# Paired mixer banks for DeltaNet's heads, norms summed by ScalarE, layer norm in parts, and steps placed anew

## The chip, the cores and the metric

One Trainium2 chip, one of its NeuronCores. The time is the device time of one execution of the kernel in microseconds (us); a kernel's time is the median of its runs. Engines are named as in the profile: PE (TensorE's matmuls), PEld (its weight loads), DVE (VectorE), ACT (ScalarE), POOL (GpSimd), SP (SyncE, which starts most DMAs).

## The reference

Two residual layers on x of 256 tokens x 2048, float32, with 256 memory tokens. Each layer is one input projection of the RMS-normed stream, token mixers on slices of it, a gate for each, and one output projection:

```
even:  p = rms_norm(h) @ w_in                      (2048 x 9232)
  A) q,k,v = silu(causal_conv(p[:3072], 4 taps)), 8 heads of 128
     q,k = l2_norm(q)/sqrt(128), l2_norm(k);  gated delta rule in chunks of 64
     o_a = rms_norm(o) * silu(z_a)
  B) glu = a * sigmoid(b) (1024 wide); c = causal_conv(glu, 31 taps) + bias
     o_b = silu(layer_norm(c)) * silu(z_b)
  M) 4 heads of softmax attention over the memory, times silu(z_m)
  h = h + concat(o_a, o_b, o_m) @ w_out            (3072 x 2048)
odd:   stick-breaking attention (16 heads) and the memory attention, gated,
  h = h + concat(o_c, o_m) @ w_out
```

## The kernel before

**The products.** The weights of all projections are cut into 432 chunks of 256 rows by 512 columns. Each is loaded once by SP into one of six `raw` buffers (`load_chunk`, L716). ACT rounds it to `whi` (L912), DVE takes the remainder `wlo` (L1245), both into rings of seven, and PE multiplies it by the two 128-token halves of x, itself kept as a rounded part `xhi` and a remainder `xlo`: three products for each (L1608, L1609, L1610), 12 matmuls of 128x512 for a chunk, into four PSUM banks. This "job" work goes on from the first microsecond to the last, and PE does the mixers' small products and transpositions (`turn`, L1647) between two chunks.

**The order.** `make_plan` (L155) writes one list of steps for all engines. Position p is the place ahead of chunk p; `stream(k, pos, items)` puts steps from a position on, each item with the distance to the next. Each engine walks through the whole list and does its own part of a step (`do_<step>`), in order, so an engine that waits inside a step holds back everything behind it. The split of a chunk (L912 on ACT, L1245 on DVE) stands 4 positions ahead of its products (`AHEAD`). The 124 tap steps of the 31-tap convolution (L1469, on DVE) are put wherever DVE's estimated time leaves room: `VECTOR_SHARE` and `TENSOR_SHARE` hold estimates in chunks, `CONV_SHARE` is that of a tap step, and `CONV_ROOM` what DVE may be behind.

**Mixer banks.** Four more PSUM banks `M[0]` to `M[3]` take the mixers' results. `banks(step)` (L581) says which a step uses; `take` lets PE wait until the last reader of each is through.

**DeltaNet** (`deltanet(g)`, four heads at a time). For a head: `dnT`, PE turns q, k and v (six blocks of 128x128) into banks 0 and 1; `dnC`, ACT writes the first tap of the 4-tap convolution (L1006) and DVE adds nine more (L1319); `dnS`, ACT's tanh back into banks 0 and 1 (L1012, L1013); `dnU`, DVE makes silu of it (L1327, L1329); `dnB`, POOL squares q and k (L825), PE sums the squares by four one-column products with ones (L1711) and turns k and v back by token (three blocks, L1647), all into bank 2, ACT copies the turned blocks out (L1020), DVE the norms (L1335). Then the factors (`dnV`, `dnR`, `dnG`), the inverse of the chunk's triangular matrix (`inF`, `inT`, and `d4x`/`d4y`: POOL masks a product at L851, PE multiplies at L1748, L1760 and L1762, DVE at L1416), the recurrence (`d5a` to `d5e`), the output's norm (`d6`, with ACT's accumulated squares at L1070), `gate`, and `d7`, which turns the output into the layout that the output projection reads.

**Convolution module.** `glu`, `gT` (turned, ACT's copy at L1084), the tap steps, `lnc` (POOL adds the finished channels, L859), then the layer norm: `lnm` (mean by PE, one subtraction of 2048 columns on DVE, L1476), `lnv` (ACT squares, DVE adds), `lns` and `lnr` (variance, root, reciprocal, and one multiplication of 2048 columns, L1494), `lno` (per 256 columns: gain and bias on DVE, ACT's tanh, DVE's gates).

**Others.** `zT` turns and applies gates (L1509), `xt` turns x or memory and splits it (L949 on ACT, L1266 on DVE, two banks), `mf` moves mixed results into the products' layout. SP starts, ahead of the first chunks, 14 loads of small vectors (L728).

The head loop as it was:

```
for h in range(h0, h0 + 4):
    s += [(("dnT", h), .2), (("dnC", h), 1.2), (("dnS", h), .9),
          (("dnU", h), DN_STEP - (2.1 if h > h0 else 1.7))]
    s += [(("dnB", h - 1), .1)] if h > h0 else []
```

## Time and profile before

| | |
|---|---|
| median of 3 runs | 1384.59 us (1384.58 to 1385.32) |
| the profiled execution | 1385.76 us |
| its span in the profile | 1384.0 us |
| PE busy | 1363.7 us, 99% of the span, 6473 instructions |
| DVE busy | 890.0 us, 64% |
| ACT busy | 753.1 us, 54% |
| POOL busy | 113.1 us, 8% |
| mean granted TensorE clock | 0.995 of full speed |
| DMA | 172 GB/s over the span |

The span is the time from the first to the last instruction of the profiled execution; 1.76 us of that execution lie outside it. Busy time of PE holds matmuls at the throttled clock too, so a busy PE is not one at its peak. An idle time of an engine costs the end only where PE, which has work of its own all the way, is the one that waits.

### The profile page before, as it was taken

The numbers are of one execution on the slowest core, as the hardware profiler recorded it, in microseconds if no ns is written. First come the engines' busy times: TensorE is split into PE (matmuls) and PEld (weight loads), VectorE is DVE, ScalarE is ACT, GpSimd is POOL, SyncE is SP. The second block draws the span as 40 slices with busy tenths as digits, with TensorE's granted clock in tenths as the row PEclk, the third lists the DMA queues.
The fourth block names the chain that finished last, engine by engine and source line by source line (L and its number), as shares of the span: only waits on it lengthen the run. The fifth ranks groups of instructions, "written<-read, shape, count | busy, mean of one in ns | idle before, by whom it ended". The sixth has DMA issues, their size and how long they took to land.

```text
span 1384.0 us, 17368 instructions
## 1 busy us (share of the span) xinstructions
PE 1363.7 (99%) x6473; PEld 1131.6 (82%) x6473; DVE 890.0 (64%) x1327; ACT 753.1 (54%) x1163; POOL 113.1 (8%) x112
## 2 busy tenths in 40 slices
PE   8999999999999999899999999999999999999998
PEld 7788888887888878788888888888888888888887
DVE  5457688887787888665566545654645745556563
ACT  5545543556435564665445455856756757665341
POOL 2001201012210100000000120020020100000000
PEclk9999999999999999999999999999999999999999
DMA  9655545554554675365464655464564564653652
GB/s 291 204 170 167 168 145 179 160 160 152 148 192 136 207 244 181 103 219 162 136 199 151 215 167 193 135 206 151 182 198 149 176 189 141 197 168 122 196 184 76
DMA packets 134477, 239.27 MB, mean 173 GB/s; under 512 B 13904, under 2 KB 19961, under 8 KB 134393
## 3 DMA queue, kind: packets, MB, share of 16 engines
...
HBM read 234.32 MB, written 3.80 MB: 172 GB/s over the span
## 4 chain that ended last, share of the span: by engine, by line
PE 89%; DVE 5%; issue 3%; ACT 2%; DMA 1%; POOL 0%; SPq 0%; DVEq 0%; ACTq 0%; POOLq 0%
PE job L1608 26%; PE job L1610 26%; PE job L1609 26%; PE mixer L1647 3%; DVE wlo L1245 2%; PE mixer L1856 1%; PE mixer L1876 1%; PE mixer L1748 1%; DVE reg L1319 1%; DMA raw<-in_ev_w_in_dram 1%; DVE cvr L1469 1%; PE mixer L1894 1%; PE mixer L1762 1%; PE mixer L1907 0%; PE mixer L1729 0%
## 5 line engine op out<-in xcount | busy, mean ns | idle before, releaser
L1608 PE MATMUL job<-whi,xhi 128*128 128x512 f32 x1724 | 693.4, 402 | 0.0
L1245 DVE TENSOR_TENSOR wlo<-raw,whi 128x1024 fp32r<-128x1024 f32 x432 | 528.4, 1241 | 230.5 <-ACT whi L912 228.0
L1610 PE MATMUL job<-whi,xlo 128*128 128x512 f32 x1724 | 675.6, 392 | 0.0
L1609 PE MATMUL job<-wlo,xhi 128*128 128x512 f32 x1724 | 674.0, 391 | 0.0
L912 ACT ACTIVATE whi<-raw 128x1024 fp32r<-128x1024 f32 x432 | 445.9, 1056 | 143.5 <-PE job L1610 134.9
L1610 PEld LDWEIGHTS job<-whi,xlo 128*128 128x128 f32 x1724 | 325.0, 189 | 70.5
L1609 PEld LDWEIGHTS job<-wlo,xhi 128*128 128x128 f32 x1724 | 326.0, 189 | 63.1
L1608 PEld LDWEIGHTS job<-whi,xhi 128*128 128x128 f32 x1724 | 325.4, 189 | 62.0 <-DVE xlo L1272 0.2
L1469 DVE SCALAR_TENSOR_TENSOR cvr<-cvr,vt 128x255 f32<-128x255 f32 (+14 forms) x240 | 106.9, 501 | 0.0
L939 ACT ACTIVATE proj<-job,rstd 128x512 f32<-128x512 f32 x80 | 50.5, 686 | 51.5 <-PE job L1610 44.2
L1261 DVE TENSOR_TENSOR hid<-hid,job 128x512 f32<-128x512 f32 x48 | 30.7, 681 | 50.1 <-PE job L1610 50.1
L1647 PE MATMUL mixer<-ident,proj 128*128 128x128 f32 x256 | 42.3, 273 | 5.3 <-ACT cvr L1084 2.1
L1647 PEld LDWEIGHTS mixer<-ident,proj 128*128 128x128 f32 x256 | 32.0, 140 | 17.1 <-issue 7.7
L1566 DVE SCALAR_TENSOR_TENSOR scr<-mixer,scr 128x384 f32<-128x384 f32 x16 | 8.9, 557 | 56.4 <-ACT scr L1196 56.4
L1194 ACT ACTIVATE scr<-mixer 128x384 f32<-128x384 f32 x16 | 7.9, 492 | 60.0 <-PE mixer L1894 60.0
L814 POOL TENSOR_TENSOR brs<-bss,mhalf 128x16 f32<-128x16 f32 x4 | 15.2, 3808 | 306.9 <-DVE bss L1560 306.9
L949 ACT ACTIVATE xhi<-mixer,vt 128x256 fp32r<-128x256 f32 x48 | 20.1, 470 | 31.3 <-PE mixer L1647 31.3
L1319 DVE SCALAR_TENSOR_TENSOR reg<-mixer,vt,reg 128x255 f32<-128x255 f32 (+2 forms) x72 | 28.7, 472 | 9.7 <-ACT reg L1006 9.7
L1042 ACT ACTIVATE reg<-mixer 128x512 f32<-128x512 f32 x12 | 7.2, 599 | 42.1 <-PE mixer L1748 42.1
L1121 ACT ACTIVATE mix<-mixer 128x256 f32<-128x256 f32 x40 | 15.1, 377 | 21.4 <-PE mixer L1647 21.4
L851 POOL TENSOR_TENSOR reg<-hid,mix 128x512 f32<-128x512 f32 x12 | 17.9, 1493 | 93.3 <-DVE mix L1377 59.8
L1266 DVE SCALAR_TENSOR_TENSOR xlo<-mixer,vt,xhi 128x256 fp32r<-128x256 f32 x48 | 20.8, 477 | 6.9 <-ACT xhi L949 6.9
...
## 6 DMA issues: line engine op xcount, KB each, us to landing
raw<-in_od_w_in_dram SPq DMA_DIRECT2D x160, 512.0 KB, 4.5
...
```

What stands on the lines that cost most here:

```text
L912: act(whi[:, c % RING, :, :], raw[:, c % RAWS, :, :], ACT.Copy).then_inc(s_hi, 1)
L939: ins = act(dst, pj[j % 2][t][:, :], ACT.Copy, scale=rstd[:, src, t:t + 1])
L949: act(xhi[:, SLOT[n], :], M[banks("xt", n)[0]][:, 0:S], ACT.Copy, scale=xt_gain(n)).then_inc(s_xh, 1)
L1245: vec.tensor_tensor(wlo[:, c % RING, :, :], raw[:, c % RAWS, :, :], whi[:, c % RING, :, :].bitcast(F32), ALU.subtract).then_inc(s_lo, 1)
L1261: ins = vec.tensor_tensor(v, v, pj[j % 2][t][:, :], ALU.add)
L1266: vec.scalar_tensor_tensor(out=xlo[:, SLOT[n], :], in0=M[banks("xt", n)[0]][:, 0:S], scalar=xt_gain(n), in1=xhi[:, SLOT[n], :].bitcast(F32 ...
L1319: vec.scalar_tensor_tensor(out=y[:, r:], in0=dn_source(c)[:, 0:S - r], scalar=vt[:, col:col + 1], in1=y[:, r:], op0=ALU.mult, op1=ALU.add) ...
L1469: ins = vec.scalar_tensor_tensor(out=c[:, d:], in0=gsrc[:, 0:S - d], scalar=vt[:, col:col + 1], in1=c[:, d:], op0=ALU.mult, op1=ALU.add)
L1608: mm(out_, xh, hi, start=first, stop=False)
L1609: mm(out_, xh, lo, start=False, stop=False)
L1610: return mm(out_, xl, hi, start=False, stop=last)
L1647: return nc.tensor.transpose(dst, src, ident[:, :])
```

## The change

- **Banks.** `dnT` and `dnB` of even heads use banks 0 and 1, those of odd heads 2 and 3. A head now takes 3 positions: turns and first taps at the first, the step back by token of the head before and the tanh at the second, silu at the third.
- **Norms.** POOL's squares, PE's one-column products and DVE's copy are gone. PE turns all six blocks back (q's and k's too), and ACT, behind its copy of three of them, takes four squares with an accumulated sum, straight into `nrm`.
- **Outputs.** `d7` of the first four heads stands right behind their gates and goes to banks 2 and 3.
- **Order.** `CONV_SHARE` is .33 for .36, and the `xt` and `mf` steps are placed ahead of the tap steps, so that their DVE time counts when these are levelled; sixteen `xt` steps of the memory stand one to a position, not two; `gT` and the first tap steps move by a position or two.
- **Layer norm in parts.** Subtraction, squares and sum by 512 columns; the gain and the reciprocal in one instruction for 256 columns; the bias by ACT.
- **Start.** Ten warming calls of PE for seven, the gain's transposition (`first`) inside the list behind the first split, eleven small vector loads right behind chunk 0's on SP, without the wait for the first piece of x.

The core of the diff (left out: semaphore names, the tables of steps, and where `M[0]`, `M[1]` become `M[2 * (h % 2)]` and the next):

```diff
-WARM = 7
-DN_STEP = 3.5
+WARM = 10
 BASE, LEVELS = 4, 3
 INV_STEP = (3.0, 3.0)
 CONV_ROOM = 0.2
-CONV_SHARE = 0.36
+CONV_SHARE = 0.33
 ...
-            s += [(("dnT", h), .2), (("dnC", h), 1.2), (("dnS", h), .9), (("dnU", h), DN_STEP - (2.1 if h > h0 else 1.7))]
-            s += [(("dnB", h - 1), .1)] if h > h0 else []
-        s += [("wait", 1), (("dnB", h0 + 3), 1), (("dnV", g), 2), (("dnR", g), 2.5)]
+            s += [(("dnT", h), 0), (("dnC", h), 1)] + ([(("dnB", h - 1), 0)] if h > h0 else [])
+            s += [(("dnS", h), 1), (("dnU", h), 1)]
+        s += [(("dnB", h0 + 3), 1), (("dnV", g), 2), (("dnR", g), 2.5)]
 ...
-        return s, last + [("wait", 1)] + [(("d7", h), 2 - 1.2 * g) for h in range(h0, h0 + 4)]
+        return s, last + [("wait", g)] + [(("d7", h), .5 + .3 * g) for h in range(h0, h0 + 4)]
 ...
+    stream(-1, -1, [(("first", 0), 0)])
 ...
-    start = max(int(p) + 1, after(J_V[1]))
+    start = max(int(p) + 3, after(J_V[1]))
 ...
+        stream(5, CH0[J_MEM] - 11 + k, [(("xt", F_MEM + k), 0)])
+        stream(5, CH0[J_MEM] - 2 + k, [(("xt", F_MEM + 8 + k), 0)])
 ...
-        stream(2, after(J_GLU[g] + 1) + 6 * g, [(("glu", g), 1)] + [(("gT", ct), 1) for ct in range(4 * g, 4 * g + 4)])
+        stream(2, after(J_GLU[g] + 1) + 6 * g, [(("glu", g), 2 + g)] + [(("gT", ct), 1) for ct in range(4 * g, 4 * g + 4)])
 ...
-            if p < after(J_GLU[pr // 2] + 1) + 6 * (pr // 2) + 3 + 2 * (pr % 2):
+            if p < after(J_GLU[pr // 2] + 1) + 7 * (pr // 2) + 4 + 2 * (pr % 2):
 ...
     p = stream(2, p, [(("lnm", 0), 2)])
-    p = int(p) + 1
-    stream(2, p, [(("lnv", a), 0) for a in range(4)])
-    p = stream(2, p + 2, [(("lns", 0), 0), (("lnr", 0), 2)])
-    p = stream(2, max(p, q), [(("lno", ct), .8) for ct in range(8)])
+    p = stream(2, int(p), [(("lnx", 0), .5), (("lnx", 1), .5), (("lnv", 1), .5), (("lnx", 2), .5), (("lnv", 2), .5),
+                           (("lnx", 3), .5), (("lnv", 3), 1)])
+    p = stream(2, p, [(("lns", 0), 0), (("lnr", 0), 2)])
+    p = stream(2, max(p, q), [(("lna", 0), .5)])
+    for ct in range(8):
+        p = stream(2, p, ([(("lna", ct + 1), .4)] if ct < 7 else []) + [(("lno", ct), .5)])
 ...
-        stream(5, CH0[J_MEM] + k - 2, [(("xt", F_MEM + 2 * k), 0), (("xt", F_MEM + 2 * k + 1), 0)])
 ...
-                return [1 if i in (5, 7) else 2]
+                return [2 + i % 2 if i < 4 else 1 if i in (5, 7) else 2]
+            if step in ("dnT", "dnB"):
+                return [0, 1, 2, 3][2 * (i % 2):2 * (i % 2) + 2]
 ...
-            sp.wait_ge(s_xin[0], 16)
+            for dst, src in vecs(vrow)[1:12]:
+                sp.dma_start(dst, src).then_inc(s_vrow, 16)
 ...
-            for dst, src in vecs(vrow)[1:]:
+            for dst, src in vecs(vrow)[12:]:
 ...
-            def do_dnB(h):
-                gp.wait_ge(s_silu, 2 * h + 2)
-                if h:
-                    gp.wait_ge(s_np, h)
-                k = ykqv[:, h % 4, 0:2, :]
-                nc.gpsimd.tensor_tensor(scr[:, 0:512].rearrange("p (c s) -> p c s", c=2), k, k, ALU.mult).then_inc(s_sq, 1)
 ...
-                act(tok[:, h % 4, :, :], M[2][:, 0:384].rearrange("p (c n) -> p c n", c=3), ACT.Copy).then_inc(s_tok, 1)
+                m = M[2 * (h % 2):2 * (h % 2) + 2]
+                act(tok[:, h % 4, :, :], m[1][:, 0:384].rearrange("p (c n) -> p c n", c=3), ACT.Copy).then_inc(s_tok, 1)
+                for a in range(4):
+                    v = m[0][:, 128 * a - 128:128 * a] if a else m[1][:, 0:128]
+                    ins = act(scr[:, 128 * a:128 * a + 128], v, ACT.Square, accum_out=nrm[:, h, a:a + 1])
+                ins.then_inc(s_nrm, 1)
 ...
+            def do_lnx(a):
+                sc.wait_ge(s_xc, a + 1)
+                if a >= 2:
+                    sc.wait_ge(s_lss, a - 1)
+                dst = cvr[:, 8:10, :] if a else scr[:, 512:1024].rearrange("p (c s) -> p c s", c=2)
+                act(dst, cvr[:, 2 * a:2 * a + 2, :], ACT.Square).then_inc(s_lsq, 1)
 ...
+            def do_lna(ct):
+                sc.wait_ge(s_xn, ct + 2)
+                act(cvr[:, ct, :], cvr[:, ct, :], ACT.Identity, bias=gain("ev_ln_b", ct)).then_inc(s_ly, 1)
 ...
-            def do_dnB(h):
-                ve.wait_ge(s_np, h + 1)
-                ve.wait_ge(s_tok, h + 1)
-                vec.tensor_copy(nrm[:, h, :], M[2][:, 384:388]).then_inc(s_nrm, 1)
 ...
-                v = cvr[:, 0:8, :]
-                vec.tensor_tensor(v, v, scr[:, 0:S].unsqueeze(1).broadcast_to([128, 8, S]), ALU.subtract).then_inc(s_xc, 1)
+                v = cvr[:, 2 * a:2 * a + 2, :]
+                vec.tensor_tensor(v, v, scr[:, 0:S].unsqueeze(1).broadcast_to([128, 2, S]), ALU.subtract).then_inc(s_xc, 1)
 ...
-                if a == 0:
-                    vec.tensor_copy(acc, sq).then_inc(s_lss, 1)
-                else:
-                    ve.wait_ge(s_lss, a)
-                    vec.tensor_tensor(acc, acc, sq, ALU.add).then_inc(s_lss, 1)
+                if a > 1:
+                    ve.wait_ge(s_lss, a - 1)
+                vec.tensor_tensor(acc, acc, sq, ALU.add).then_inc(s_lss, 1)
 ...
-                link(vec.reciprocal(r, r))
-                v = cvr[:, 0:8, :]
-                vec.tensor_tensor(v, v, r.unsqueeze(1).broadcast_to([128, 8, S]), ALU.mult).then_inc(s_xn, 1)
-
-            def do_lno(ct):
+                vec.reciprocal(lnacc[:, :], r).then_inc(s_xn, 1)
+
+            def do_lna(ct):
                 ve.wait_ge(s_xn, 1)
                 c = cvr[:, ct, :]
-                vec.tensor_scalar(c, c, gain("ev_ln_g", ct), gain("ev_ln_b", ct), ALU.mult, ALU.add).then_inc(s_ly, 1)
+                vec.scalar_tensor_tensor(out=c, in0=c, scalar=gain("ev_ln_g", ct), in1=lnacc[:, :], op0=ALU.mult, op1=ALU.mult
 ...
-                pe.wait_ge(s_sq, h + 1)
-                for a in range(4):
-                    ins = mm(M[2][:, 384 + a:385 + a], scr[:, 128 * a:128 * a + 128], ones[:, 0:1], start=True, stop=True)
-                ins.then_inc(s_np, 1)
+                m = M[2 * (h % 2):2 * (h % 2) + 2]
                 y = ykqv[:, h % 4, :, :]
-                turn(M[2][:, 0:128], y[:, 0, 0:128])
-                turn(M[2][:, 128:256], y[:, 2, 0:128])
-                turn(M[2][:, 256:384], y[:, 2, 128:256]).then_inc(s_back, 1)
+                turn(m[1][:, 0:128], y[:, 0, 0:128])
+                turn(m[1][:, 128:256], y[:, 2, 0:128])
+                turn(m[1][:, 256:384], y[:, 2, 128:256])
+                turn(m[0][:, 0:128], y[:, 0, 128:256])
+                turn(m[0][:, 128:256], y[:, 1, 0:128])
+                turn(m[0][:, 256:384], y[:, 1, 128:256]).then_inc(s_back, 1)
```

ACT in the first group of heads (`dnC` L1006/L1010, split L912/L911, `dnS` L1012 and L1013/L1016 and L1017, `dnB` L1020/L1025 and L1028), before:

```order
L1006 ACTIVATE reg<-mixer,vt 128x256 x3
L912 ACTIVATE whi<-raw 128x1024
L1012 ACTIVATE mixer<-reg 128x512
L1013 ACTIVATE mixer<-reg 128x256
L939 ACTIVATE proj<-job,rstd 128x512 x2
L912 ACTIVATE whi<-raw 128x1024 x2
L1020 ACTIVATE hid<-mixer 128x384
L912 ACTIVATE whi<-raw 128x1024
```

and in the change, the same stretch, one head:

```order
L1010 ACTIVATE reg<-mixer,vt 128x256 x3
L911 ACTIVATE whi<-raw 128x1024
L1025 ACTIVATE hid<-mixer 128x384
L1028 ACTIVATE scr,nrm<-mixer 128x128 x4
L1016 ACTIVATE mixer<-reg 128x512
L1017 ACTIVATE mixer<-reg 128x256
L911 ACTIVATE whi<-raw 128x1024
L943 ACTIVATE proj<-job,rstd 128x512 x2
L911 ACTIVATE whi<-raw 128x1024
```

The copy for the head before now stands ahead of this head's tanh, with four squares behind it.

POOL where the second four heads' blocks are inverted (a memset of `inF`, `lnc` L859/L858, mask products of `d4x` L851/L850, the power of `d6` L814/L820), before:

```order
L831 MEMSET mix 64x16
L859 TENSOR_TENSOR lnacc<-lnacc,cvr 128x256 x2
L851 TENSOR_TENSOR reg<-hid,mix 128x512 x6
L859 TENSOR_TENSOR lnacc<-lnacc,cvr 128x256 x2
L814 TENSOR_TENSOR oms<-oms,mhalf 128x8
```

and in the change:

```order
L830 MEMSET mix 64x16
L850 TENSOR_TENSOR reg<-hid,mix 128x512 x4
L858 TENSOR_TENSOR lnacc<-lnacc,cvr 128x256 x2
L850 TENSOR_TENSOR reg<-hid,mix 128x512 x2
L820 TENSOR_TENSOR oms<-oms,mhalf 128x8
```

Two additions of the sum for the layer norm have moved from ahead of the six mask products to a place ahead of the last two.

DVE at the layer norm (splits L1245, `xlo` of `xt` L1266, sums L1482 and L1485, L1490 to L1494 the variance's part), before:

```order
L1482 COPY scr<-cvr 128x512
L1485 TENSOR_TENSOR scr<-scr,cvr 128x512 x3
L1266 SCALAR_TENSOR_TENSOR xlo<-mixer,vt,xhi 128x256 x2
L1245 TENSOR_TENSOR wlo<-raw,whi 128x1024
L1266 SCALAR_TENSOR_TENSOR xlo<-mixer,vt,xhi 128x256 x2
L1245 TENSOR_TENSOR wlo<-raw,whi 128x1024
L1490 TENSOR_SCALAR scr<-mixer 128x256
L1492 RECIPROCAL scr<-scr 128x256
L1494 TENSOR_TENSOR cvr<-cvr,scr 128x2048
L1266 SCALAR_TENSOR_TENSOR xlo<-mixer,vt,xhi 128x256 x2
```

and in the change (splits L1254, `xlo` L1278, subtraction L1483, sums L1490, the variance's part L1495 and L1497):

```order
L1254 TENSOR_TENSOR wlo<-raw,whi 128x1024
L1490 TENSOR_TENSOR scr<-scr,cvr 128x512
L1483 TENSOR_TENSOR cvr<-cvr,scr 128x512
L1278 SCALAR_TENSOR_TENSOR xlo<-mixer,vt,xhi 128x256
L1254 TENSOR_TENSOR wlo<-raw,whi 128x1024
L1490 TENSOR_TENSOR scr<-scr,cvr 128x512
L1278 SCALAR_TENSOR_TENSOR xlo<-mixer,vt,xhi 128x256
L1254 TENSOR_TENSOR wlo<-raw,whi 128x1024
L1495 TENSOR_SCALAR scr<-mixer 128x256
L1497 RECIPROCAL lnacc<-scr 128x256
```

The long instructions and the four sums in a row have been cut and stand with a split or two between them.

## Rows read from the trace of the kernel before

**Rows 1.** The page, part 4: the chain that ended last, by engine.

```profile
PE 89%; DVE 5%; issue 3%; ACT 2%; DMA 1%; POOL 0%; SPq 0%; DVEq 0%; ACTq 0%; POOLq 0%
```

**Rows 2.** Waits of PE, 96 to 570 us: us in total, times, longest us.

```profile
PE mixer L1647 <- DVE xlo L1266: 4.0, 2, 2.1
PE mixer L1647 <- ACT cvr L1084: 2.1, 2, 1.9
PE mixer L1647 <- DVE mix L1509: 1.9, 2, 1.4
PE mixer L1647 <- DVE reg L1329: 1.2, 2, 0.9
PE mixer L1748 <- issue: 1.0, 1, 1.0
```

**Rows 3.** Timeline of PE: start us, us, instructions, [idle before <-releaser].

```profile
340.92 0.41 PE L1647 MATMUL mixer<-ident,proj 128*128 128x128 f32 x2 [1.88 <-ACT cvr L1084]
...
492.94 0.39 PE L1610 MATMUL job<-whi,xlo 128*128 128x512 f32 x1
493.79 0.41 PE L1647 MATMUL mixer<-ident,proj 128*128 128x128 f32 x2 [0.46 <-DVE mix L1509]
...
567.54 0.66 PE L1647 MATMUL mixer<-ident,reg 128*128 128x128 f32 x2 [2.14 <-DVE xlo L1266]
```

**Rows 4.** Windows: us, busy us of each engine, PEclk, DMA share, GB/s.

```profile
97.30:144.30 47.00, 46.08 (x227) 38.70 (x226) 36.69 (x61) 27.38 (x42) 4.95 (x3) 1.00 0.54 160
557.00:561.00 4.00, 4.00 (x12) 3.10 (x12) 2.93 (x4) 2.72 (x4) 0.00 (x0) 0.57 0.42 129
700.00:720.00 20.00, 20.00 (x90) 16.57 (x89) 13.16 (x20) 9.31 (x14) 0.00 (x0) 1.00 0.62 199
```

**Rows 5.** Timeline of PE: a head's turns, and a step back by token.

```profile
97.34 0.82 PE L1647 MATMUL mixer<-ident,proj 128*128 128x128 f32 x6
97.92 0.48 PE L1608 MATMUL job<-whi,xhi 128*128 128x512 f32 x1
...
144.34 0.95 PE L1711 MATMUL mixer<-ones,scr 128*128 128x1 f32 x8
145.43 0.47 PE L1608 MATMUL job<-whi,xhi 128*128 128x512 f32 x1
```

**Rows 6.** Timeline of DVE in the layer norm.

```profile
541.81 2.29 DVE L1476 TENSOR_TENSOR cvr<-cvr,scr 128x2048 f32<-128x2048 f32 x1 [0.77 <-ACT scr L1089]
...
564.71 2.29 DVE L1494 TENSOR_TENSOR cvr<-cvr,scr 128x2048 f32<-128x2048 f32 x1
```

**Rows 7.** Timelines of DVE and POOL: splits beside POOL's squares, and without them.

```profile
120.98 1.99 DVE L1245 TENSOR_TENSOR wlo<-raw,whi 128x1024 fp32r<-128x1024 f32 x1
...
126.40 1.21 DVE L1245 TENSOR_TENSOR wlo<-raw,whi 128x1024 fp32r<-128x1024 f32 x1
...
119.94 1.95 POOL L825 TENSOR_TENSOR scr<-reg 128x512 f32<-128x512 f32 x1 [10.76 <-DVE reg L1329]
```

**Rows 8.** Groups of ACT, L1070 of d6: count, busy us, mean ns.

```profile
L1070 ACT ACTIVATE hid<-hid 128x128 f32<-128x128 f32 x8 | 2.4, 302 | 7.2 <-DVE hid L1427 7.2
L1070 ACT ACTIVATION_READ_ACCUMULATOR hid<-hid 128x1 f32 x8 | 1.5, 187 | 0.0
```

**Rows 9.** Timelines of POOL, DVE and PE in the inversion of the second heads.

```profile
373.60 2.54 POOL L859 TENSOR_TENSOR lnacc<-lnacc,cvr 128x256 f32<-128x256 f32 x2 [25.89 <-DVE cvr L1469]
...
412.39 1.46 POOL L851 TENSOR_TENSOR reg<-hid,mix 128x512 f32<-128x512 f32 x1 [3.30 <-DVE mix L1416]
...
412.23 2.68 DVE L1469 SCALAR_TENSOR_TENSOR cvr<-cvr,vt 128x248 f32<-128x248 f32 x4
...
416.77 1.11 PE L1748 MATMUL mixer<-mix,reg 128*128 128x128 f32 x8
```

**Rows 10.** Timelines of ACT and PE at the start.

```profile
18.03 1.06 ACT L912 ACTIVATE whi<-raw 128x1024 fp32r<-128x1024 f32 x1 [1.65 <-DMA raw<-in_ev_w_in_dram]
...
20.89 0.65 PE L1647 MATMUL mixer<-ident,hid 128*128 128x128 f32 x4 [2.00 <-DVE xlo L1266]
```

85 lines of the change are left out of this document (42 added, 43 removed).

## The prediction

> **What bounds the kernel now.** I read first the chain that ended last, then PE's waits, then the timeline around each wait, and windows for the clock. The chain is PE for 89% of the span [rows 1], and PE has its own products from end to end, so the time changes only by what leaves or enters PE's own queue, by idle time of PE, and by its clock. Between 96 and 570 us five groups of waits add up to 4.0 + 2.1 + 1.9 + 1.2 + 1.0 = 10.2 us, in nine waits [rows 2]: the reader is to see that all end with work of the mixers, on DVE or ACT, and none with a weight's split or a load. After 600 us PE is busy throughout (20.00 of 20.00 us in a sample [rows 4]), and from there on the order of both kernels is the same, so the odd layer is worth nothing here.
>
> A wait costs a little more than its idle time. Products start .23 us apart; where 492.94 is followed by a turn at 493.79, .85 - .23 = .62 us are lost, and the row says .46 [rows 3]: .16 for the restart. And three of the waits have a second price. From 557.0 to 561.0 PE does 12 instructions in 4 us, and the granted clock is 0.57 of full speed, that is mostly the lower level (1.2 GHz) [rows 4]; it follows the wait of 1.9 us that ended at 556. Such stretches of about 3.4 us, half of it lost, 1.7 us, stand behind the waits of 1.88 us at 340.92 and of 2.14 us at 567.54 too [rows 3], and one behind the wait of 2.00 us at 20.89 [rows 10]; the waits of up to 1.4 us have none behind them. So a wait of 2 us costs 3.9 us, and one of 1.4 us costs 1.6.
>
> **The change part by part.**
>
> *Norms.* Before, a step back by token takes from 144.34 to 145.43, 1.09 us: four one-column products and three turns [rows 5]. Six turns take from 97.34 to 97.92, .58 us [rows 5]; the step now has six turns. 8 heads x (1.09 - .58) = 4.1 us leave PE's own queue. I take 4.0. This is the surest term, since nothing hides PE's work. POOL's squares go as well: beside one of 1.95 us a split of DVE took 1.99 us in place of 1.21 [rows 7], up to 8 x .78 us that DVE gets back; DVE's copy of .15 us goes too. DVE's time counts only through PE's waits, below.
>
> ACT pays: four squares with their sums, 4 x (302 + 187) ns = 1.96 us a head [rows 8]. In the four heads from 97.3 to 144.3 us ACT was busy 27.4 us beside PE's 47 [rows 4], with 15 splits in it. The change takes 12 positions for them, so about 12 splits: 27.4 - 3 x 1.06 + 4 x 1.96 = 32.1 us, against 12 x 2.73 + 8 x .58 = 37.4 us of PE. It fits. What stands behind the squares in ACT's queue is the tanh, which DVE's nine taps hold back anyway (the taps are at work for 3.5 us behind ACT's first tap, and the squares fill 2.45 us of that with the copy), then splits that are 4 chunks, 11 us, ahead of PE. Cost: nothing; without that cover it is a rival.
>
> *Paired banks.* The turns of a head waited until DVE's silu of the head before had left banks 0 and 1 (reg L1329, 1.2 us in two waits [rows 2]). Now they need the banks of the head before that one, whose last reader is an ACT square a whole head, 3 positions, earlier. Both waits go: 1.2 + 2 x .16 = 1.5 us. The group gets shorter in positions, but every chunk has to be done anyway, so this in itself is worth nothing.
>
> *Order.* The waits for ACT's copy of `gT` (2.1), for DVE's gates of `zT` (1.9) and for the mask product of `d4x` (1.0) are places where DVE or ACT had fallen behind its list; the levelling with .33 for .36 and with the `xt` and `mf` steps counted spreads the taps more evenly, `gT` moves by two positions, `zT` by eight. Adding up durations by position from the groups, I find DVE up to 4.8 us behind at the layer norm before, and under 2 us in the change, everywhere. 5.0 + 5 x .16 = 5.8 us.
>
> *Layer norm in parts.* DVE's two long instructions take 2.29 us each [rows 6], and between them stood four sums that each waited for ACT's squares. `xlo` of the paired `xt` steps, and so PE's next turn, stood behind: the waits of 1.9 and 2.1 us. Cut in four, a subtraction is some .6 us with a split between, the `xt` steps come one to a position, and the bias is ACT's. Both waits should go: 4.0 + 2 x .16 = 4.3 us.
>
> *Clock.* With the waits of 1.88, 1.9 and 2.14 us go three stretches: 3 x 1.7 = 5.1 us.
>
> *What is new.* Two additions on POOL now stand ahead of the last two mask products of the second group. They took 2.54 us [rows 9], and can start only when the last tap of their channels is done; taps start at 412.23 just as POOL starts its product of 1.46 us at 412.39, and PE takes that product at 416.77 [rows 9]. With one tap (.7) and the additions ahead, the product would end at 413.0 + 2.5 + 1.5 = 417.0: .3 late. Bounds: 0 (the taps done one position earlier) and 1.5 (the additions again slowed by DVE, as splits were [rows 7]). I take .4. The mean of the layer norm and the gates of `zT` at new places: .4, between 0 and 1. Together .8.
>
> *Start.* Three more warming calls (some .5 us each at the lower clock, estimated from 128-column turns) and `first` behind the split delay the gain by about 1 us; eleven small loads on SP ahead of the second chunk's cost its issue up to 4.6 us, less the wait removed. Against it, they no longer stand behind the loads. But what PE waits for here is chunk 4, whose split starts at 18.03 when its load has landed [rows 10], with the DMA queues full from 7 to 24 us whatever the order. Net 0, between -2.4 and +.7; the half-speed stretch behind it stays.
>
> The Trainium skill bears on one place. The DVE row beside POOL's squares shows 1.99 for 1.21 us, and POOL's additions took 2.54 for two at 373.60. "Advanced Engine Details and Errata", VectorE Performance Modes, says that VectorE's second port is shared with GpSimd and that the two block each other. By this trace the two do hinder each other; by the rule read strictly, the two additions at their new place would stall by as long as the taps run, which is the second case below.
>
> **Sum.** -4.0 - 1.5 - 5.8 - 4.3 - 5.1 + .8 = -19.9 us. The profiled execution took 1385.76 us (1.8 above its span); that gives 1365.9. The median of the runs is 1.17 us lower, 1384.59, which gives 1364.7. **Forecast: 1365.0 us**, 1.4% less. A measurement of this kernel can tell about 0.2%, 2.8 us, from no change; all of the cases but two are outside that.
>
> **Rivals.**
> - *POOL is jammed in the inversion.* The additions and DVE's taps and splits lengthen each other, and PE waits 2 us for the mask product, with a slow stretch behind (1.7): 1365 + 3.7 - .1 = 1368.6. For it: rows 7 and 9. Against it: it needs the additions to begin a position late. Chance .15.
> - *The start gets better too.* If the wait of 2.00 us at 20.89 [rows 10] falls under 1.4, its slow stretch goes: 1365 - .6 - 1.7 = 1362.7. For it: small loads out of the way of chunks 6 and 7. Against it: the first chunks get later instead. Chance .10.
> - *The stalls only move.* DVE's load is the same but for some 7 us, so half of the 11.6 us of waits and half of the slow stretches turn up at other positions (denser heads, `xt` steps one to a position beside taps): 1365 + 5.8 + 2.6 + 1.5 = 1374.9. For it: DVE and ACT waits are set by single chains, which sums by position don't see. Against it: the largest are from long instructions that no longer exist. Chance .11.
> - *PE's saved work is refilled.* The one-column products were taken out, but PE then waits for ACT's squares and nothing of the rest goes: within 3 us of 1384.6. Chance .02.
> - *Slower: ACT becomes the bound of the heads.* ACT's chain for one head is first taps 1.4, split 1.06, wait for the turns back, copy and squares 2.45, tanh .97, two splits 2.1, in order, 8.0 us and what it waits; PE's head period falls to 3 x 2.73 + 2 x .58 = 9.35 us. If the waits between come to over 1.35 us a head, ACT falls behind; when that has eaten the 11 us by which splits are ahead, PE waits. With waits of 4 us (before, ACT waited for the taps up to 3.5 us a head), that is 2.7 us a head, 8 x 2.7 = 22, and 8 slow stretches of 1.7, 13: 1365 + 35 = 1400. Against it: only four heads stand in a row, so 11 us are hardly eaten; and the squares lie in the wait rather than behind it. Chance .04.
>
> **How the numbers follow.** Main case .58; with the rivals .15, .10, .11, .02, .04. The main case by itself reaches from 1361.5 (start at -2.4, new terms 0) to 1369 (new terms at 2.5, waits that stay short). The range runs from 1360.5 to 1372; left out are the moved stalls, the refilled work and the slower case, .17. Faster by over 0.2%: .58 + .15 + .10 + .11 = .94, less .01 for what I haven't thought of: .93. Within 0.2%: .03. Slower: .04.
>
> **What would show it.** PE's instructions: 8 x 4 one-column products gone, and the group of a step back and a head's turns, both between two chunks, takes 1.16 us. Waits of PE from 96 to 570 us: 10.2 us before, under 1.5 after, the ones on `reg` and `xlo` gone. Granted clock 1.00 in windows from 96 to 570 us, and the slow stretch after 21 us still there. POOL's additions near the end of the second group, and a mask product PE waits for by no more than .5 us. Of ACT: squares ahead of each tanh, and less idle time ahead of the tanh than before. I am wrong if PE shows a wait of over 1.5 us with a slow stretch behind it anywhere in the even layer, if the step back by token costs PE more than .6 us, or if the odd layer has changed.

## The result, and the profile after

| | before | the change |
|---|---|---|
| median | 1384.95 us (1384.58 to 1385.53, 4 runs) | 1376.58 us (1375.62 to 1378.61, 4 runs) |
| the profiled execution, its span | 1385.76, 1384.0 us | 1378.61, 1376.9 us |

The ratio is 0.9941, with an interval from 0.9924 to 0.9958: faster by 8.4 us, where 20 were forecast. The median lies outside the range of 1360.5 to 1372.

The page of the change: busy time of each engine, and the chain that ended last.

```profile
PE 1356.5 (99%) x6439; PEld 1123.8 (82%) x6439; DVE 883.9 (64%) x1320; ACT 764.3 (56%) x1235; POOL 98.5 (7%) x104
...
PE 76%; DVE 2%; ACT 1%; issue 1%; POOL 0%; DVEq 0%; ACTq 0%; POOLq 0%
```

The shares of this chain add up to 80%, those of [rows 1] to 100%: the rest of it wasn't followed, so the two can't be compared share by share. PE has 34 records fewer and is busy 7.2 us less; ACT has the squares (753.1 us before, 764.3 now). The waits of PE from 96 to 600 us (us in total, times, longest), which answer to [rows 2]:

```profile
PE job L1614 <- DVE wlo L1254: 3.1, 3, 1.8
PE mixer L1830 <- DVE scr L1490: 2.6, 1, 2.6
PE mixer L1824 <- POOL lnacc L858: 1.3, 1, 1.3
PE mixer L1653 <- DVE proj L1537: 0.9, 1, 0.9
PE mixer L1653 <- DVE hid L1452: 0.6, 1, 0.6
PE mixer L1653 <- DVE reg L1341: 0.5, 2, 0.3
PE mixer L1653 <- DVE mix L1516: 0.5, 1, 0.5
PE mixer L1758 <- issue: 0.4, 1, 0.4
```

They add up to 9.9 us, against 10.2 before. But the list is another: `reg` is down from 1.2 to .5 us, `gT`'s is gone, `zT`'s fell from 1.9 to .5, and the `xlo` waits are gone from this stretch. In their place stand waits at lines that PE had never waited for: the split's remainder `wlo` (L1254), the last sum of the layer norm (L1490), POOL's last addition to the mean (L858), the scaled keys (L1537). The prediction's sign for being wrong, a wait of over 1.5 us with a slow stretch behind it in the even layer, is there: 2.6 us for the last sum, and its clock below; and so is what it had seen nowhere before, waits for a weight's split.

Where the time went can be read without any model, since the records hold the start of each of the 5184 products: chunk n starts at a time in one kernel and at another in the other.

| stretch, by chunk | before | the change | difference | forecast |
|---|---|---|---|---|
| start to 27 (first head) | 97.92 | 96.82 | -1.1 | 0 |
| 27 to 148 (DeltaNet, taps) | 411.79 | 400.60 | -11.2 | -12.6 |
| 148 to 166 (mean, squares, variance) | 62.41 | 60.81 | -1.6 | } -7.3 |
| 166 to 180 (gates of the layer norm) | 39.08 | 45.87 | +6.8 | } |
| 180 to 431 (the odd layer and the rest) | 765.44 | 765.40 | 0.0 | 0 |

So the head stage did what was forecast, within 1.4 us, and the layer norm did the opposite: 5.2 us longer instead of 7.3 shorter. Of the 12.8 us between the forecast sum (-19.9) and this pair of profiles (-7.1) 12.5 arise there. (The forecast's 12.6 are the norms 4.0, banks 1.5, order 5.8 and one slow stretch 1.7, less .4 of new cost; its 7.3 the layer norm 4.3 and two slow stretches 3.4, less .4.)

A step back by token, six turns (PE's timeline; start, us):

```profile
108.51 0.82 PE L1653 MATMUL mixer<-ident,reg 128*128 128x128 f32 x6
109.08 0.47 PE L1614 MATMUL job<-whi,xhi 128*128 128x512 f32 x1
```

From 108.51 to 109.08 it takes .57 us, where [rows 5] had 1.09.

**A ring in the gates.** A ring is a cycle of hand-overs: engine A gives B something, B gives something back, and A's next round stands behind that. First DVE, then ACT, in the layer norm's gates of the change (L1254 and L911 are a chunk's split; L1502 DVE's gain times reciprocal; L1113 and L1117 ACT's bias and tanh; L1509, L1511 DVE's gates):

```profile
575.12 1.22 DVE L1254 TENSOR_TENSOR wlo<-raw,whi 128x1024 fp32r<-128x1024 f32 x1 [2.33 <-ACT whi L911]
576.26 0.48 DVE L1502 SCALAR_TENSOR_TENSOR cvr<-cvr,vt,lnacc 128x256 f32<-128x256 f32 x1
576.65 0.42 DVE L1509 SCALAR_TENSOR_TENSOR cvr<-cvr 128x256 f32<-128x256 f32 x1
577.11 0.43 DVE L1511 SCALAR_TENSOR_TENSOR mix<-cvr,mix 128x256 f32<-128x256 f32 x1
578.71 1.23 DVE L1254 TENSOR_TENSOR wlo<-raw,whi 128x1024 fp32r<-128x1024 f32 x1 [1.18 <-ACT whi L911]
```

```profile
576.77 0.51 ACT L1113 ACTIVATE cvr<-cvr,vt 128x256 f32<-128x256 f32 x1 [1.69 <-DVE cvr L1502]
577.31 0.42 ACT L1117 ACTIVATE cvr<-cvr 128x256 f32<-128x256 f32 x1
577.64 1.04 ACT L911 ACTIVATE whi<-raw 128x1024 fp32r<-128x1024 f32 x1
580.37 0.51 ACT L1113 ACTIVATE cvr<-cvr,vt 128x256 f32<-128x256 f32 x1 [1.69 <-DVE cvr L1502]
```

The reader is to see two idle times that answer each other. ACT waits 1.69 us for DVE's L1502 ahead of each bias; DVE waits 1.18 us for ACT's `whi` ahead of each split. In the order of the list, DVE's L1502 stands behind its split, which needs ACT's `whi`; and ACT's bias needs L1502 and stands ahead of ACT's next `whi`. So of this cycle no two parts overlap (only DVE's gates run beside ACT's bias): `whi` 1.0, split 1.1, L1502 .4, bias .5, tanh .4 and the hand-overs make 578.71 - 575.12 = 3.59 us a position, while PE needs 2.73. Neither engine is full. Splits are four chunks ahead, about 11 us, and over these positions that lead is used up, by .86 us a position and by 3.9 us once, for two long squares of the memory that ACT does in the middle of it. Then PE waits for `wlo`.

**Another in the squares.** DVE and ACT (L1490 sum, L1483 subtraction, L1278 `xlo`; L1105 square, L953 `xhi`):

```profile
543.53 1.23 DVE L1254 TENSOR_TENSOR wlo<-raw,whi 128x1024 fp32r<-128x1024 f32 x1 [0.46 <-ACT whi L911]
544.67 0.68 DVE L1490 TENSOR_TENSOR scr<-scr,cvr 128x512 f32<-128x512 f32 x1
545.27 0.68 DVE L1483 TENSOR_TENSOR cvr<-cvr,scr 128x512 f32<-128x512 f32 x1
547.02 0.48 DVE L1278 SCALAR_TENSOR_TENSOR xlo<-mixer,vt,xhi 128x256 fp32r<-128x256 f32 x1 [1.06 <-ACT xhi L953]
547.96 1.23 DVE L1254 TENSOR_TENSOR wlo<-raw,whi 128x1024 fp32r<-128x1024 f32 x1 [0.46 <-ACT whi L911]
```

```profile
545.99 0.63 ACT L1105 ACTIVATE cvr<-cvr 128x512 f32<-128x512 f32 x1 [2.49 <-DVE cvr L1483]
546.52 0.46 ACT L953 ACTIVATE xhi<-mixer,vt 128x256 fp32r<-128x256 f32 x1
546.88 1.05 ACT L911 ACTIVATE whi<-raw 128x1024 fp32r<-128x1024 f32 x1
```

Split, sum, subtraction, then ACT's square, `xhi` and `whi`: 547.96 - 543.53 = 4.43 us a position where PE needs 2.9. PE waits 2.63 us for the last sum.

The clock behind these waits (windows; PEclk is the column behind POOL's):

```profile
550.00:556.00 6.00, 6.00 (x23) 4.84 (x24) 4.88 (x6) 2.60 (x5) 0.00 (x0) 0.76 0.59 178
592.00:600.00 8.00, 6.99 (x26) 5.45 (x27) 7.07 (x7) 5.54 (x9) 0.00 (x0) 0.79 0.57 168
```

.76 and .79 of full speed, a part of each stretch at the lower level (1.2 GHz), 1.5 and 1.6 us lost: so much sooner does the chunk behind come where the same wait has no such stretch behind it (e1 and e2, last section).

### The profile page after: what moved, and what is told of

It reads as the page before. It is cut to its first block, busy times and chain, and to the rows that moved or that the text cites. A ratio compares the mean times of both kernels' runs of the same rounds, so it can differ in the third digit from the quotient of the medians.

```text
span 1376.9 us, 17340 instructions
## 1 busy us (share of the span) xinstructions
PE 1356.5 (99%) x6439; PEld 1123.8 (82%) x6439; DVE 883.9 (64%) x1320; ACT 764.3 (56%) x1235; POOL 98.5 (7%) x104
## 4 chain that ended last, share of the span: by engine, by line
PE 76%; DVE 2%; ACT 1%; issue 1%; POOL 0%; DVEq 0%; ACTq 0%; POOLq 0%
PE job L1614 22%; PE job L1616 22%; PE job L1615 22%; PE mixer L1653 3%; PE mixer L1866 1%; PE mixer L1886 1%; ACT whi L911 1%; DVE wlo L1254 1%; PE mixer L1904 1%; PE mixer L1917 1%; PE mixer L1758 0%; PE mixer L1903 0%; PE mixer L1918 0%; PE mixer L1772 0%; PE mixer L1739 0%
## 5 line engine op out<-in xcount | busy, mean ns | idle before, releaser
L1254 DVE TENSOR_TENSOR wlo<-raw,whi 128x1024 fp32r<-128x1024 f32 x432 | 526.8, 1236 | 246.2 <-ACT whi L911 243.7
L911 ACT ACTIVATE whi<-raw 128x1024 fp32r<-128x1024 f32 x432 | 445.5, 1055 | 135.0 <-PE job L1616 123.9
L1653 PEld LDWEIGHTS mixer<-ident,proj 128*128 128x128 f32 x256 | 32.3, 140 | 11.1 <-DVE proj L1537 1.3
L953 ACT ACTIVATE xhi<-mixer,vt 128x256 fp32r<-128x256 f32 x48 | 20.8, 468 | 29.5 <-PE mixer L1653 29.5
L820 POOL TENSOR_TENSOR brs<-bss,mhalf 128x16 f32<-128x16 f32 x4 | 15.2, 3806 | 306.9 <-DVE bss L1567 306.9
L1278 DVE SCALAR_TENSOR_TENSOR xlo<-mixer,vt,xhi 128x256 fp32r<-128x256 f32 x48 | 21.5, 477 | 11.1 <-ACT xhi L953 10.6
L1198 ACT ACTIVATE cvr<-mixer,qgain 128x256 f32<-128x256 f32 x16 | 7.6, 475 | 31.4 <-PE mixer L1653 31.4
```

The source lines that it names most:

```text
L911: act(whi[:, c % RING, :, :], raw[:, c % RAWS, :, :], ACT.Copy).then_inc(s_hi, 1)
L953: act(xhi[:, SLOT[n], :], M[banks("xt", n)[0]][:, 0:S], ACT.Copy, scale=xt_gain(n)).then_inc(s_xh, 1)
L1254: vec.tensor_tensor(wlo[:, c % RING, :, :], raw[:, c % RAWS, :, :], whi[:, c % RING, :, :].bitcast(F32), ALU.subtract).then_inc(s_lo, 1)
L1278: vec.scalar_tensor_tensor(out=xlo[:, SLOT[n], :], in0=M[banks("xt", n)[0]][:, 0:S], scalar=xt_gain(n), in1=xhi[:, SLOT[n], :].bitcast(F32 ...
L1653: return nc.tensor.transpose(dst, src, ident[:, :])
```

## The experiments

All are edits of the change unless said otherwise, three rounds each with the kernel before on the same chip (e14: five). The kernel before had medians of 1382.9 to 1384.6 us there (single runs 1381.2 to 1386.7), and the change's median was taken beside another chip's 1384.95, so that differences of medians can be off by 1 to 2 us. Besides them I go by the difference of chunk starts. Outside of an edited place it agrees to .15 us from chunk 27 to 148, but not at the start of a run (up to 1.5 us) nor where one execution has a slow stretch and the other has none (1.5 or 1.6 us). "Aligned" is that difference to the profiled execution of the change, which lies 2.0 us above the median of the change: 1.6 us of it is the slow stretch at 592, which some executions don't have.

### e1: the gates' ring apart

```diff
-    p = stream(2, max(p, q), [(("lna", 0), .5)])
-    for ct in range(8):
-        p = stream(2, p, ([(("lna", ct + 1), .4)] if ct < 7 else []) + [(("lno", ct), .5)])
+    p = stream(2, max(p, q) - 1, [(("lna", 0), 1)])
+    for ct in range(8):
+        p = stream(2, p, ([(("lna", ct + 1), 0)] if ct < 7 else [])
+                   + [(("lnt", ct), 0), (("lno", ct), .9)])
 ...
-            def do_lna(ct):
+            def do_lnt(ct):
                 sc.wait_ge(s_xn, ct + 2)
```

(The function is ACT's; DVE's `do_lna` stays, a position earlier than its `do_lno`.)

> Edit against the change: ACT's bias and tanh of a channel stand one position behind DVE's multiplication by gain and reciprocal (a step of its own), all else equal. Theory R (ring of hand-overs): in the gates of the layer norm each position runs ACT's split, DVE's split, DVE's multiplication, ACT's bias and tanh one after the other, 3.59 us a position in the trace of the change against PE's 2.73, until the splits' lead is used up and PE waits 4.0 us at chunks 174 to 178 (with a slow stretch behind, 6.8 us in all). Then this edit takes the ring apart: 1376.6 - 6 = about 1370.5, and ACT's idle time of 1.69 us before each bias is gone. Rival B (too much work): ACT and DVE simply have too much to do there (3.85 us of the memory's squares among it); the order of hand-overs does not matter: 1376.6 within 1.5.

Measured: 1372.24 us (1370.41 to 1372.82), ratio to before .9912 (.9892 to .9932). DVE, then ACT:

```profile
572.25 1.22 DVE L1254 TENSOR_TENSOR wlo<-raw,whi 128x1024 fp32r<-128x1024 f32 x1
573.38 0.48 DVE L1502 SCALAR_TENSOR_TENSOR cvr<-cvr,vt,lnacc 128x256 f32<-128x256 f32 x1
573.78 0.42 DVE L1509 SCALAR_TENSOR_TENSOR cvr<-cvr 128x256 f32<-128x256 f32 x1
574.23 0.42 DVE L1511 SCALAR_TENSOR_TENSOR mix<-cvr,mix 128x256 f32<-128x256 f32 x1
574.57 1.22 DVE L1254 TENSOR_TENSOR wlo<-raw,whi 128x1024 fp32r<-128x1024 f32 x1
```

```profile
573.90 0.51 ACT L1113 ACTIVATE cvr<-cvr,vt 128x256 f32<-128x256 f32 x1 [0.42 <-DVE cvr L1502]
574.44 0.42 ACT L1117 ACTIVATE cvr<-cvr 128x256 f32<-128x256 f32 x1
```

A position takes 574.57 - 572.25 = 2.32 us, ACT's idle time ahead of the bias is .42 for 1.69, with not one instruction less. PE's waits for `wlo` and for the keys are gone; aligned, chunks 174 to 178 take 6.8 us less, of which 1.6 are the slow stretch of that one execution; the ring itself cost 5.2. The medians are 4.3 us apart, 1.7 less than expected, and far outside B's 1.5. The memory's squares stand where they stood: theory R holds, B falls. Whether the ring would use up the lead without those squares no run shows.

### e2: the squares' ring apart

```diff
-    (("lnx", 0), .5), (("lnx", 1), .5), (("lnv", 1), .5), (("lnx", 2), .5), (("lnv", 2), .5),
-    (("lnx", 3), .5), (("lnv", 3), 1)
+    (("lnx", 0), 0), (("lnx", 1), 1), (("lnq", 0), 0), (("lnq", 1), 0), (("lnx", 2), 0),
+    (("lnv", 1), 1), (("lnq", 2), 0), (("lnx", 3), 0), (("lnv", 2), 1), (("lnq", 3), 0), (("lnv", 3), 1)
 ...
-            def do_lnx(a):
+            def do_lnq(a):
```

(ACT's squares; DVE's subtraction stays `do_lnx`.)

> Edit against the change: ACT's squares of the layer norm stand one position behind DVE's subtraction, DVE's sums behind them. Theory R: the same ring at the squares, with the split, sum, subtraction, square and xhi one behind the other, is 4.43 us a position against PE's 2.9; the edit takes out PE's wait of 2.63 us for the last sum and the slow stretch behind it: 1376.6 - 4 = 1372.6, and perhaps more if the gates then start with a larger lead. Rival B: the work is the same, 1376.6 within 1.5.

Measured: 1373.44 us (1372.40 to 1373.95), ratio .9922 (.9903 to .9941). DVE at the same place:

```profile
541.51 1.22 DVE L1254 TENSOR_TENSOR wlo<-raw,whi 128x1024 fp32r<-128x1024 f32 x1
542.64 0.69 DVE L1483 TENSOR_TENSOR cvr<-cvr,scr 128x512 f32<-128x512 f32 x1
543.25 0.69 DVE L1490 TENSOR_TENSOR scr<-scr,cvr 128x512 f32<-128x512 f32 x1
543.85 0.48 DVE L1278 SCALAR_TENSOR_TENSOR xlo<-mixer,vt,xhi 128x256 fp32r<-128x256 f32 x1
544.25 1.22 DVE L1254 TENSOR_TENSOR wlo<-raw,whi 128x1024 fp32r<-128x1024 f32 x1
```

No idle time, 544.25 - 541.51 = 2.74 us a position for 4.43. The wait for the last sum is gone; aligned, chunks 162 to 166 take 4.4 us less, of which 1.5 are a slow stretch that e1 and e7 lack with the wait in place. The gates stay as they were: the waits there are the same three and the same 1.8 us at most, so the lead regained didn't save them.

### e3: both

> Edit against the change: the two edits of e1 and e2 together. Theory R (rings of hand-overs): aligned by chunk, the edit at the squares took 4.0 us out of chunks 162 to 166 and that at the gates 6.8 us out of chunks 174 to 178; they are apart, so both come: 1376.6 - 10.7 = 1365.9, which is also what the prediction had for the change as a whole. Rival (shared lead): the lead regained at the squares is what saved the gates, so the second edit adds little: 1371.

Measured: 1367.40 us (1367.04 to 1367.84), ratio .9882 (.9868 to .9897). Aligned, -4.4 and -6.8 both appear, 11.1 us together, to a few hundredths what e2 and e1 gave. They add; there is no shared lead. The median is 1.5 us over the expectation, since the 6.8 hold the stretch of 1.6 us that some executions of the change lack.

### e9: and the mean a position later

```diff
-    p = stream(2, p, [(("lnm", 0), 2)])
+    p = stream(2, p + 1, [(("lnm", 0), 1)])
```

> Edit against e3: the mean of the layer norm (PE's product with ones) a position later, the subtractions where they were. PE waits 1.26 us for POOL's last addition there, 1.4 us with the restart. Theory W (POOL's two additions, 2.51 us behind the last tap, decide): the wait goes, e3 - 1.4 = 1364.5. Rival: DVE's subtraction then waits for the mean (PE, then ACT's copy) and carries the delay on to the squares and the last sum: e3 within .5.

Measured: 1365.65 us (1365.09 to 1365.70), ratio .9869 (.9854 to .9883). What waits PE still has from 96 to 600 us:

```profile
PE mixer L1653 <- DVE hid L1452: 0.5, 1, 0.5
PE mixer L1653 <- DVE reg L1341: 0.5, 2, 0.3
PE mixer L1653 <- DVE mix L1516: 0.5, 1, 0.5
PE mixer L1758 <- issue: 0.3, 1, 0.3
```

1.8 us, and none over .5. The wait for POOL went without another behind it.

### e4: the layer norm as before

The functions `do_lnm`, `do_lnv`, `do_lnr`, `do_lno` and the rule for their places are those of the kernel before (the places themselves come a position sooner, since the taps end a position sooner); the rest is the change.

> Edit against the change: the layer norm's steps as before (one subtraction, one multiplication of 2048 columns, four sums in a row, gain and bias on DVE), all else as in the change. The prediction's step (layer norm in parts takes two waits and two slow stretches away, 7.7 us): 1376.6 + 7.7 = 1384.3. Theory R: the layer norm in parts made the stretch from chunk 148 to 180 5.2 us longer (101.5 us before, 106.7 in the change), so the old one gives 1371.4. A middle case, that the single xt steps already help the old layer norm: 1368.

Measured: 1370.84 us (1370.11 to 1371.25), ratio .9903 (.9881 to .9925). The part of the change that was to speed up this stage slowed it, with the `xt` steps one to a position beside it, by 5.7 us; the prediction's own step would have had 1384.3 here, theory R 1371.4. The old layer norm has its own loss here: PE waits 2.0 us for `xlo`, and chunks 166 to 168 take 3.8 us longer than in the change. Its gates have a ring too, but ACT's part of it is the tanh alone: 568.09 - 565.11 = 2.98 us a position (DVE's splits), .25 over PE's 2.73 in place of .86, and PE doesn't wait there.

### e7: DVE's and POOL's part of the memory's norms apart

```diff
     stream(5, CH0[J_MEM] + 6, [(("rstd", 1), 0)])
+    stream(5, CH0[J_MEM] + 8, [(("rstv", 1), 0)])
```

(`rstv` is DVE's and POOL's part.)

> Edit against the change: of the memory's row norms, ACT's two long squares stay at their position (3.8 us), DVE's and POOL's part behind them stands two positions later, so DVE no longer idles 3.9 us for them ahead of its split. Theory R: the ring stays, so the lead is still used up, only later: 1376.6 - 2, between 0 and -4. Rival B (the block of work is what counts): ACT's block is still there: 1376.6 within 1.

Measured: 1377.20 us (1376.19 to 1378.11), ratio .9950 (.9931 to .9969). No gain: PE waits for `wlo` four times, 3.7 us, for three times and 3.1. DVE's single stop of 3.9 us isn't what uses up the lead; ACT's block stays in this run. The number is within B's range and .6 us over the end of R's, which is inside the noise: R's 2 us of gain didn't come, and the run doesn't tell R from B.

### e5: the norms as before

POOL's squares, PE's one-column products and DVE's copy as before, in the paired banks; no squares on ACT.

```diff
+                pe.wait_ge(s_sq, h + 1)
+                for a in range(4):
+                    ins = mm(m[1][:, 384 + a:385 + a], scr[:, 128 * a:128 * a + 128], ones[:, 0:1], ...)
-                turn(m[0][:, 0:128], y[:, 0, 128:256])
-                turn(m[0][:, 128:256], y[:, 1, 0:128])
-                turn(m[0][:, 256:384], y[:, 1, 128:256]).then_inc(s_back, 1)
```

> Edit against the change: the norms as before (POOL's squares, four one-column products of PE, DVE's copy), in the paired banks, all else as in the change. The prediction's term: 8 x .51 us more on PE, 1376.6 + 4.1 = 1380.7. Rival 1: PE waits for POOL's squares (1.6 to 2 us behind the silu), or DVE slowed by POOL turns up as waits: 1383 or more. Rival 2: the squares on ACT cost as much as they save, 1376.6 within 1.

Measured: 1385.44 us (1384.11 to 1387.59, 10 runs), ratio 1.0011 (1.0001 to 1.0021). Aligned, each step back costs .50 to .52 us more, 4.1 in all: the prediction's term to a tenth. And rival 1 is right as well:

```profile
PE mixer L1732 <- POOL scr L833: 3.5, 2, 1.8
```

at the last head of each group, 1.57 us more each, since there the step back follows the silu by one position, and POOL's squares of 1.95 us lie between. By chunk 100 that makes 7.2 us. The medians are 8.9 us apart; where the other 1.7 come from stays open.

### e13: the banks not paired

```diff
             if step in ("dnT", "dnB"):
-                return [0, 1, 2, 3][2 * (i % 2):2 * (i % 2) + 2]
+                return [0, 1] if step == "dnT" else [2, 3]
```

> Edit against the change: all heads' turns in banks 0 and 1, the steps back in 2 and 3, positions as in the change. In the change the silu of a head ends .3 to 1.0 us after the next head's turns begin (106.05 against 105.09, 114.89 against 114.64). Theory P (the pair of banks is what lets PE go on): each of six turns waits, .94 + 2 x .25 and three restarts of .16 in the first group, about as much in the second: 1376.6 + 3.5 = 1380. The prediction's term: 1.5 us, 1378.1. Rival (the spacing by itself does it): 1376.6 within 1.

Measured: 1381.03 us (1378.73 to 1381.99, 10 runs), ratio .9974 (.9965 to .9984). PE's waits for silu, 96 to 400 us:

```profile
PE mixer L1653 <- DVE reg L1341: 2.6, 6, 1.0
```

Six waits, as theory P has it; aligned, 3.4 us more from chunk 27 to 90 (the medians are 4.5 apart). At three positions to a head the pair is worth twice what the waits of before showed.

### e8: the start as before

```diff
-WARM = 10
+WARM = 7
 ...
-            for dst, src in vecs(vrow)[1:12]:
-                sp.dma_start(dst, src).then_inc(s_vrow, 16)
+            sp.wait_ge(s_xin[0], 16)
```

and all small loads behind the weights'.

> Edit against the change: seven warming calls, the wait for the first piece of x and all small vector loads behind the weights' again. In the trace of the change chunk 8 starts .9 us earlier than before. If that is from the order of the loads: 1376.6 + .9 = 1377.5. The prediction had this part at net 0 (the loads are bound by the DMA queues): 1376.6 within .5, and the start of a run varies by up to 1.5 us by itself.

Measured: 1376.72 us (1375.43 to 1378.37), ratio .9950 (.9935 to .9966). No difference. In its profile chunk 8 starts 1.1 us later than in that of the change, but in e14's, with the change's start, it does so by .5 us; and chunk 27, 1.3 us later in e8, is 1.5 later in e1. A gain of a few tenths is not excluded.

### e11, e15: the memory's `xt` steps in pairs; and the layer norm held in place

```diff
-        stream(5, CH0[J_MEM] - 11 + k, [(("xt", F_MEM + k), 0)])
-        stream(5, CH0[J_MEM] - 2 + k, [(("xt", F_MEM + 8 + k), 0)])
+        stream(5, CH0[J_MEM] + k - 2, [(("xt", F_MEM + 2 * k), 0), (("xt", F_MEM + 2 * k + 1), 0)])
```

and in e15 besides:

```diff
-    p = stream(2, p, [(("lnm", 0), 2)])
+    p = stream(2, max(p, 158), [(("lnm", 0), 2)])
```

> Edit against the change: the memory's xt steps in pairs from position 158 on, as before. Theory R: two xhi and two xlo lie in each position of the squares' ring, .8 us more on each turn of it: the wait at the last sum grows from 2.6 to about 5 us: 1376.6 + 3 = 1379.6. Rival (one to a position or two is the same): 1376.6 within 1.

> Edit against e11 (the memory's xt steps in pairs): the layer norm held at its positions of the change, 158 for the mean, where e11 had let it start at 156, two positions sooner. Theory R: with the pairs in the ring of the squares each turn of it is .8 us longer, so PE waits 4 to 6 us for the last sum and the gates' ring is as in the change: 1376.6 + 3 = 1379.6. Rival (pairs cost nothing, e11's 1373.6 came from the pairing itself): 1373.6 within 1.

Measured: e11 1373.60 us (1372.75 to 1374.47), ratio .9923 (.9908 to .9937); e15 1375.51 us (1375.05 to 1376.31), ratio .9939 (.9924 to .9954). Against theory R's number for e11, 3 us faster and not slower. I had overlooked that the taps end two positions sooner, and with them the layer norm begins. With it held back, e15, two thirds of the gain is gone, but the number is 4 us under R's: the squares' ring is 4.8 us (541.48 to 546.28) for 4.43, not .8 longer, PE's waits are 1.8 and 1.4 us, for pairs of turns and not for the last sum, and its wait of 1.3 us for the mean is gone, since the taps end three positions ahead of it. That the gates are as in the change is right: the same waits of .57, 1.86, .84 and .69 us. In e11 the gates' ring is as long (its splits start at 566.80 and 570.40), but it begins two positions sooner against the memory's squares, which stay, and PE waits there once, 1.73 us, for 4.0 in all: what a ring costs hangs on the lead that is left when it begins.

### e10, e16: CONV_SHARE .36; and the same with both rings apart

```diff
-CONV_SHARE = 0.33
+CONV_SHARE = 0.36
```

> Edit against the change: CONV_SHARE .36 for .33. The tap steps end at position 164 for 157, so the layer norm starts seven positions later, at 165, behind all the memory's xt steps. Theory R (rings): at the squares the ring loses xhi's part (.46 and .36 us) and is about 3.6 us for 4.4, so of the 2.6 us wait at the last sum less than 1 us is left, but the gates' ring stays 3.6 us long: 1376.6 - 4 = 1372.6. The prediction's theory (the levelling with .33 is what removed waits): waits for gT and zT are back, 1376.6 + 4 = 1381.

> Edit against e10 (CONV_SHARE .36, which puts the layer norm seven positions later, at the memory's squares and the first turns of its keys): both rings taken apart as in e3. Theory R: the waits of 7.6 us (keys' turns for ACT) and of 5.3 us (last sum) are the rings' delays plus the memory's 3.9 us block; without the rings most of the 7.6 goes and some 2 us of the 5.3 is left: 1386.7 - 11 = 1375.5, within 2. Rival (work is crowded there, whatever the order of hand-overs): 1384 or more.

Measured: e10 1386.66 us (1385.27 to 1387.67, 10 runs), ratio 1.0019 (1.0009 to 1.0028); e16 1368.85 us (1367.98 to 1369.49), ratio .9889 (.9872 to .9905). PE's waits from 380 to 640 us, first e10, then e16:

```profile
PE mixer L1653 <- ACT reg L1160: 7.6, 1, 7.6
PE mixer L1830 <- DVE scr L1490: 5.3, 1, 5.3
PE mixer L1758 <- POOL reg L850: 1.7, 1, 1.7
PE mixer L1653 <- DVE proj L1537: 0.5, 1, 0.5
```

```profile
PE mixer L1758 <- POOL reg L850: 1.7, 1, 1.7
```

Neither number for e10 was right. No wait for `gT` or `zT` is back, but the taps end at position 164 for 157, and the layer norm, seven positions later, meets the memory's squares ahead of its own and the turns of the memory's keys (L1160) behind: PE needs those at their position, they are no longer four chunks ahead of anything, and the gates' ring holds ACT up by 7.6 us. With the rings apart and nothing else moved, 17.8 us are gone, more than the 11 expected; the waits of 7.6 and 5.3 us disappear entirely. This is the sharpest test of R against "too much work in one place": the work, and the place of the stage, are the same.

### e14: the best version

e9 with one more position ahead of the first four outputs' turns (`last + [("wait", 1)]` for both groups).

> Edit against e9 (both rings apart, the mean a position later): the first four outputs' turns a position later behind their gates. PE waits .55 us for the first gate there, .7 us with the restart: if the gate is late by less than a position, e9 - .7 = 1365.0; if the wait only moves to the next step, 1365.65 within .3.

Measured: 1365.26 us (1364.83 to 1365.78), ratio .9862 (.9848 to .9877), 11.3 us under the change. The wait for the gate is gone, and chunk 100 starts .8 us sooner after chunk 44 than in e9; between the medians of e9 and e14 the difference isn't resolved.

## Why the prediction was wrong

**Read rightly.** That only PE's own queue, its waits and its clock count, and that the odd layer is worth nothing, held: 0.0 us over the last 252 chunks. *Norms*: 4.0 predicted; e5 shows 4.1, and 3.1 us more by a way not named there, a wait for POOL that the closer spacing would have brought. *Paired banks*: 1.5 predicted; e13 shows 3.4, since the closer heads would have waited more. Both terms were read from the old spacing; e5 and e13 measure the parts at the new one, so what they show above the terms is no gain over the kernel before and isn't in the sum. *Order*, up to chunk 148: nearly right, with 2.0 us of small waits in their place (`hid` .6, `reg` .5, `mix` .5, issue .4) that had no term. *POOL's two additions* in the inversion: .4 predicted, no wait at all. The jam, a rival at .15, was one position away: in e10 the first of them comes at 112 for 111, and there PE waits 1.7 us for POOL's product, 3.5 with the slow stretch behind. What the Trainium skill has in "Advanced Engine Details and Errata", VectorE Performance Modes, that instructions of GpSimd and those of VectorE that use its second port block each other, decided nothing there; the trace agrees with it at the layer norm's mean, below, where two additions of POOL take 2.51 us beside a split and 1.61 without. *Start*: 0 predicted, and e8 agrees within what it can tell; but the half-speed stretch that was to stay isn't in the change's profile (granted 1.00 from 20 to 26 us, .72 before), and it is in those of e5 and e14, with the same start: it comes and goes by itself. *ACT's squares* cost nothing, as said: ACT stood ahead of the tanh anyway, and was busy 26.8 of 37.5 us there, for the 32.1 of the prediction, which added up squares that overlap (last section).

**The step that failed** is "Layer norm in parts ... Both waits should go: 4.3 us", and with it "*Clock*", 3.4 of its 5.1 us. The two waits for `xlo` did go. But the change puts in their place rings with 3.59 and 4.43 us a position, and PE waits 2.6 us for the last sum and 4.0 us in the gates, with a slow stretch behind each in this execution. The ground of the mistake stands one part earlier: "Adding up durations by position ... I find DVE up to 4.8 us behind at the layer norm before, and under 2 us in the change, everywhere." Nothing here speaks against that sum, but it doesn't decide: by sums, the gates need 2.4 us of DVE and 1.9 of ACT a position, both under 2.73. By the chain, they need 3.59. The rival "The stalls only move" gave this very reason ("DVE and ACT waits are set by single chains, which sums by position don't see") and 1374.9, not far from 1376.6; but it was argued as a loss of half everywhere, with 1.5 us in it that it gives no source for, and not taken to the diff; that its number came near is luck. There it could have been seen in two lines: `do_lna` gave ACT an instruction that needs DVE's of the same position, ahead of the next `whi`. "The bias is ACT's" stands in the prediction as relief. (A slip that changes nothing: of the prediction's six cases one, not two, lies within 2.8 us of no change.)

Also missing was the wait of 1.3 us for the mean. POOL's last two additions, before and in the change:

```profile
537.42 1.61 POOL L859 TENSOR_TENSOR lnacc<-lnacc,cvr 128x256 f32<-128x256 f32 x2 [42.62 <-DVE cvr L1469]
```

```profile
526.08 2.51 POOL L858 TENSOR_TENSOR lnacc<-lnacc,cvr 128x256 f32<-128x256 f32 x2 [64.29 <-DVE cvr L1476]
```

In both kernels PE's product stands one position behind the last tap. Before, the additions took 1.61 us, with DVE idle for the first 1.1 of them, and PE didn't wait; in the change a split of DVE begins with them (525.92), they take 2.51 us, and PE waits 1.26.

With the two rings apart and the mean later, the change gives 1365.65 (e9), where the prediction had 1365.0. By stage, against the profile before: start -1.3 for 0, chunks 27 to 148 -11.3 for -12.6, layer norm -7.5 for -7.3, the rest 0. So once the rings aren't there the layer norm is worth what was said, and the rest of the agreement is in part luck: a start that varies by as much makes up for the head stage.
